# Norms through one root per token, and a modulation summed on VectorE, in a two-block transformer kernel

## The reference

```python
def rmsnorm(x, g):
    y = x * rsqrt(mean(x * x, axis=-1) + EPS)
    return y * g

mod = silu(c) @ w_ada.T + b_ada               # 6 x 1024 values, w_ada is 6144 x 1024
sh1, sc1, gt1, sh2, sc2, gt2 = split(mod, 6)

h = rmsnorm(x, g_mix) * (1 + sc1) + sh1       # norm "first"
proj = h @ w_in                               # q, k, v, pooling, gated convolution
attn = diff_attention(q, k, v)                # 8 heads of 64
attn = rmsnorm(attn, g_subln) * 0.8           # per head: "subln"
x = x + gt1 * (concat(attn, pool, conv) @ w_out)
h = rmsnorm(x, g_ffn) * (1 + sc2) + sh2       # norm "ffn"
x = x + gt2 * (silu(gate) * up) @ w_down
x = rmsnorm(x, g_final)                       # norm "final"

h = rmsnorm(x, g_norm1)                       # norm "second"
# three attentions: fox, swa, and one over 256 memory rows:
mn = rmsnorm(mem, g_mem)                      # norm "mem"
mk, mv = split(mn @ w_mem_kv, 2)
x = x + merged @ w_out_2
x = x + peer_ffn(rmsnorm(x, g_norm2))         # norm "peer", experts picked by top-k
```

## Time and profile before

| | |
|---|---|
| runs, us | 2722.94, 2724.3, 2726.37 (median 2724.3) |
| profiled execution, us | 2727.47, its span 2725.7 |
| TensorE busy | 2557.2 us, 94% |
| VectorE busy | 1528.9 us, 56% |
| ScalarE busy | 725.1 us, 27% |
| GpSimd busy | 1786.2 us, 66% |
| mean granted TensorE clock | 0.970 |

### The profile page before, as it was taken

How to read it: one execution, slowest core, us unless ns; L and a number is a source line. 1 busy time by engine, 2 the same in 40 slices (tenths; PEclk the granted TensorE clock), 3 DMA queues, 4 the chain that set the end, 5 groups by cost and what they waited for, 6 DMA issues and landing times.

```text
span 2725.7 us, 35334 instructions
## 1 busy us (share of the span) xinstructions
PE 2557.2 (94%) x12644; PEld 2132.2 (78%) x12644; DVE 1528.9 (56%) x3197; ACT 725.1 (27%) x1297; POOL 1786.2 (66%) x1315
## 2 busy tenths in 40 slices
PE   3989799999989999998889998999999989999999
PEld 2866568888757666677768898999999978888887
DVE  5447632121246325445438898877778366666665
ACT  5148511000132323433310111111212123333332
POOL 2746557666824243366556676999998668888885
PEclk8989899999989999999999998999999999999999
DMA  6224222222311011122223345899987799999995
GB/s 245 93 70 148 101 77 93 93 103 98 108 48 62 31 47 66 47 92 79 78 81 118 119 146 197 291 366 357 345 337 296 273 365 346 342 341 352 352 353 219
DMA packets 134761, 502.61 MB, mean 184 GB/s; under 512 B 11248, under 2 KB 53872, under 8 KB 103152
## 3 DMA queue, kind: packets, MB, share of 16 engines
q1 hardware_dynamic: 70832, 311.97, 31.4%
q0 software_dynamic: 36864, 134.23, 13.0%
q10 hardware_dynamic: 26944, 54.85, 5.3%
HBM read 448.58 MB, written 52.43 MB: 184 GB/s over the span
## 4 chain that ended last, share of the span: by engine, by line
PE 61%; DVE 11%; POOL 10%; DMA 9%; issue 5%; ACT 3%; ACTq 0%; SPq 0%; DVEq 0%; POOLq 0%
PE banks L566 9%; PE banks L567 9%; PE banks L568 9%; DMA raw<-weights 4%; POOL W_lo L503 3%; POOL W_lo L426 3%; PE banks L694 3%; DMA B_lo_plain<-u_rows,arena 3%; PE banks L924 2%; PE banks L926 2%; PE banks L925 2%; PE banks L839 2%; PE banks L841 2%; PE banks L840 2%; PE banks L712 2%
## 5 line engine op out<-in xcount | busy, mean ns | idle before, releaser
L451 POOL TENSOR_TENSOR W_lo<-raw,W_hi 128x512 fp32r<-128x512 f32 x376 | 493.9, 1323 | 0.0
L454 POOL TENSOR_TENSOR beat<-zero 128x1 f32<-128x1 f32 x94 | 19.8, 211 | 615.8 <-PE banks L714 215.5
L839 PE MATMUL banks<-A_hi,W_hi 128*128 128x384 f32 x1024 | 381.0, 372 | 1.2 <-issue 1.1
L841 PE MATMUL banks<-A_hi,W_lo 128*128 128x384 f32 x1024 | 346.4, 338 | 0.0
L840 PE MATMUL banks<-A_lo,W_hi 128*128 128x384 f32 x1024 | 344.5, 336 | 0.0
L426 POOL TENSOR_TENSOR W_lo<-raw,W_hi 128x2048 fp32r<-128x2048 f32 x65 | 299.4, 4606 | 5.2
L566 PE MATMUL banks<-A_hi,W_hi 128*128 128x512 f32 x680 | 267.8, 394 | 4.9 <-issue 4.9
L568 PE MATMUL banks<-A_hi,W_lo 128*128 128x512 f32 x680 | 264.7, 389 | 0.0
L567 PE MATMUL banks<-A_lo,W_hi 128*128 128x512 f32 x680 | 264.6, 389 | 0.0
L446 POOL CAST W_hi<-raw 128x512 fp32r<-128x512 f32 x376 | 247.9, 674 | 0.0
L1877 DVE TENSOR_TENSOR A_lo<-arena,A_hi 128x768 fp32r<-128x768 f32 x64 | 136.6, 2134 | 171.5 <-ACT A_hi L1362 171.4
(11 more groups left out here) (282 smaller groups left out, 6185.0 us busy)
## 6 DMA issues: line engine op xcount, KB each, us to landing
raw<-weights SPq DMA_DIRECT2D x241, 1024.0 KB, 4.9
gelu_dram<-B_plain ACTq DMA_DIRECT2D x64, 384.0 KB
gates_dram<-arena ACTq DMA_DIRECT2D x48, 512.0 KB, 10.0
arena<-gelu_dram SPq DMA_DIRECT2D x32, 768.0 KB, 8.4
arena<-gates_dram SPq DMA_DIRECT2D x32, 768.0 KB, 11.1
W_plain<-weights SPq DMA_DIRECT2D x4, 1024.0 KB, 15.9
X<-x_t SPq DMA_DIRECT2D x1, 2048.0 KB, 14.4
arena<-v_rows,arena POOLq DMA_INDIRECT x128, 7.9
```

The lines of the kernel that those rows point to most:

```text
L451: return pool.tensor_tensor(W_lo[:, j, cols], raw[:, j, cols], W_hi[:, j, cols].bitcast(F32), ALU.subtract)
L839: mm(to, lh, rh, start=k == 0, stop=False)
L841: last = mm(to, ll, rh, start=False, stop=k == KD - 1)
```

## The change

**Roots.** TensorE now takes the block of 128 tokens of a square as the stationary operand and one column of mean_all as the moving one (`norm_sums`), four matmuls of one column for each of the eight squares: the mean stands once per token, tokens on the partitions, in 128 x 4 values. ScalarE's root and VectorE's reciprocal work on these, in `roots`, a part of `small` in SBUF. `norm_spread` brings them back over features by tokens: the column of a block, broadcast to 128 columns, is stationary, and the identity streams (128 columns). VectorE's products wait for it (`root_spread`). In "mem" the spread stands behind the slab on A. "subln" becomes one such group for all eight heads: 16 matmuls of two columns, one root and one reciprocal of 128 x 32 values, and 32 spreads of 64 x 128, which stand between the two halves of the `behind_split`; VectorE multiplies and splits tile by tile behind them. The other head norms stay.

**First modulation.** All eight slabs have places of their own (four in the arena, two each in B and B_lo) and are issued at once, X behind the first; the first two slabs of w_in follow into raw without a wait. VectorE multiplies a half slab by silu(c), which ScalarE leaves in PSUM, and sums it in the same instruction; ScalarE has no part in it. VectorE's reciprocal of "first" stands before the last slab. The biases are copied to PSUM. The split of w_forget moves behind the norm, the exponential of lambda to the end of the stage before the difference attention. Behind the first spread four matmuls of 512 columns are added that nobody reads (`HEAD_BUSY`).

```diff
+HEAD_BUSY = 4
-        small = sb("small", [P, 56])
+        small = sb("small", [P, 88])
+        roots = small[:, 56:88]
...
+        ada_places = [at(4096 + SLAB * i, SLAB) for i in range(4)] + \
+            [t[:, 4 * i:4 * i + 4, :].rearrange("p a b -> p (a b)") for t in (B_plain, B_lo_plain) for i in range(2)]
+        c_psum = two_banks[0][:, :]
+        def head_root(b, i):
+            return bank[(6, 7, 5 - b, 4 + b)[i]]
...
@@ sync
-            for s in range(2):
-                sp.dma_start(raw[:, s, :], stream[s, :, :]).then_inc(slab_loaded[s], 16)
-            sp.dma_start(X[:, :, :], x_in.rearrange("(k p) t -> p k t", p=P)).then_inc(const_loaded, 16)
-            for s in range(4):
-                sp.dma_start(W_plain[:, s, :], stream[2 + s, :, :]).then_inc(ada_loaded[s], 16)
+            for s in range(ADA_FIRST):
+                sp.dma_start(ada_places[s], stream[s, :, :]).then_inc(ada_loaded[s], 16)
+                if s == 0:
+                    sp.dma_start(X[:, :, :], x_in.rearrange("(k p) t -> p k t", p=P)).then_inc(const_loaded, 16)
-            for s in range(6, ADA_FIRST + 2):
-                sp.wait_ge(ada_used, s - 5 if s < ADA_FIRST else s - 1)
+            for s in range(ADA_FIRST, ADA_FIRST + 2):
                 load_slab(s, s % 2)
@@ tensor
-            def behind_split(which, ks=range(KD), waits=range(KD), n_slabs=1, stride=256):
+            def behind_split(which, ks=range(KD), waits=range(KD), n_slabs=1, stride=256, ahead=None):
...
                 for k in ks:
+                    if ahead and k == waits[0]:
+                        ahead()
...
-            def norm(name):
-                n = NORMS[name][1]
+            def norm_sums(name):
+                blocks = NORMS[name][1] // P
                 b = work()
                 for k in range(KD):
                     take(norm_square)
-                    last = mm(bank[4 + b][:, 0:n], mean_all, S[k % 4][:, 0:n], start=k == 0, stop=k == KD - 1)
+                    for q in range(blocks):
+                        last = mm(bank[4 + b][:, q:q + 1], S[k % 4][:, P * q:P * q + P], mean_all[:, 0:1],
+                                  start=k == 0 and q == 0, stop=k == KD - 1, skip_group_check=True)
                     if k < 4:
                         last.then_inc(square_summed, 1)
                 last.then_inc(work_ready[b], 1)
+                return b, blocks
+
+            def norm_spread(b, blocks):
+                take(root_inverted)
+                for q in range(blocks):
+                    last = mm(bank[4 + b][:, P * q:P * q + P], roots[:, q:q + 1].to_broadcast([P, P]), ident,
+                              start=q == 0, stop=True, skip_group_check=True)
+                last.then_inc(root_spread, 1)
+
+            def norm(name):
+                norm_spread(*norm_sums(name))
...
             norm("first")
+            for _ in range(HEAD_BUSY):
+                mm(bank[2][:, :], mean_all, tab[:, :], start=True, stop=True, skip_group_check=True)
             behind_split("A")
...
-            for _ in head_norm("subln"):
-                pass
-            behind_split("B", ks=(4, 5, 6, 7, 0, 1, 2, 3), waits=range(4))
+            b = work()
+            for i in range(4):
+                take(square_ready)
+                for q in range(QT):
+                    last = mm(bank[4 + b][:, 8 * i + 2 * q:8 * i + 2 * q + 2], S[i][:, P * q:P * q + P], mean_64[:, 0:P:HD],
+                              start=i == 0 and q == 0, stop=True, skip_group_check=True)
+            last.then_inc(work_ready[b], 1)
+            def spread_heads():
+                take(root_inverted)
+                for i in range(4):
+                    for q in range(QT):
+                        for r in range(2):
+                            at_head = 8 * i + 2 * q + r
+                            last = mm(head_root(b, i)[HD * r:HD * r + HD, P * q:P * q + P],
+                                      roots[:, at_head:at_head + 1].to_broadcast([P, HD]), ident,
+                                      start=q == 0, stop=True, skip_group_check=True)
+                    last.then_inc(root_spread, 1)
+            behind_split("B", ks=(4, 5, 6, 7, 0, 1, 2, 3), waits=range(4), ahead=spread_heads)
...
-                    norm("mem")
+                    sums = norm_sums("mem")
                     features_on_partitions("A", 1)
+                    norm_spread(*sums)
                     stage()
@@ scalar
-                act.activation(bank[4 + w % 2][:, 0:n], bank[4 + w % 2][:, 0:n], ACT.Sqrt, bias=small[:, 0:1])\
+                act.activation(roots[:, 0:n // P], bank[4 + w % 2][:, 0:n // P], ACT.Sqrt, bias=small[:, 0:1])\
                     .then_inc(root_ready, 1)
...
-            for s in range(2):
-                modulation(s)
...
-            for s in range(2, ADA_FIRST):
-                modulation(s)
...
+            act.activation(small[:, 4:6], small[:, 2:4], ACT.Exp).then_inc(small_done, 1)
             loaded()
             stage_end()
@@ vector
-                step(dve.reciprocal(root, root))
+                dve.reciprocal(roots[:, 0:n // P], roots[:, 0:n // P]).then_inc(root_inverted, 1)
                 if before:
                     before()
+                take(root_spread)
...
+            def first_modulations(*slabs):
+                for s in slabs:
+                    dve.wait_ge(ada_loaded[s], 16)
+                    for m in range(2):
+                        w = ada_places[s][:, D * m:D * m + D]
+                        dve.scalar_tensor_tensor(out=w, in0=w, scalar=1.0, in1=c_psum, op0=ALU.mult, op1=ALU.mult,
+                                                 accum_out=mod[:, 2 * s + m:2 * s + m + 1])
...
-            head_norm("subln")
-            for i in range(4):
-                dve.drain().then_inc(whole_ready, 1)
-            split(4, lambda i: Ot[:, i, :], "B")
+            take(root_ready)
+            dve.reciprocal(roots, roots).then_inc(root_inverted, 1)
+            for i in range(5):
+                if i < 4:
+                    take(root_spread)
+                    o = Ot[:, i, :]
+                    dve.scalar_tensor_tensor(out=o, in0=o, scalar=small[:, 8 + i:9 + i], in1=head_root(w % 2, i)[:, :],
+                                             op0=ALU.mult, op1=ALU.mult).then_inc(whole_ready, 1)
+                if i >= 1:
+                    rest(i - 1, Ot[:, i - 1, :], "B", 0)
```

More of the change, by code:

```diff
@@ L228, in build @@
         slab_loaded = [sem("slab_loaded0"), sem("slab_loaded1")]
-        ada_loaded = [sem(f"ada_loaded{i}") for i in range(4)]
+        ada_loaded = [sem(f"ada_loaded{i}") for i in range(ADA_FIRST)]
         ada_used = sem("ada_used")
@@ L436, in split_whole, with split @@
                 low_of(s)
-            def split(s, j, ada=N_ADA - 4):
+            def split(s, j, ada=N_ADA - ADA_FIRST):
                 pool.wait_ge(slab_loaded[j], s * 8 + (8 * ada + 16))
@@ L1117, in _ @@
             silu_of_c(1)
-            for s in range(2):
-                modulation(s)
             act.wait_ge(const_loaded, 16 * 3)
             take(small_ready)
-            act.activation(small[:, 4:6], small[:, 2:4], ACT.Exp).then_inc(small_done, 1)
+            squares("first")
+            norm("first")
+            stage_end()
             act.activation(wf_hi[:, :, :], c_("w_forget", 0, 64).rearrange("p (k h) -> p k h", k=KD), ACT.Copy)\
                 .then_inc(small_done, 1)
-            squares("first")
-            for s in range(2, ADA_FIRST):
-                modulation(s)
-            norm("first")
-            stage_end()
             load(dist, "distance")
@@ L1160, in _ @@
             stage_end()
-            for _ in head_norm("subln"):
-                pass
+            for i in range(4):
+                act.activation(S[i], Ot[:, i, :], ACT.Square).then_inc(square_ready, 1)
+            w = at_["work"]
+            at_["work"] += 1
+            act.wait_ge(work_ready[w % 2], w // 2 + 1)
+            act.activation(roots, bank[4 + w % 2][:, 0:32], ACT.Sqrt, bias=small[:, 0:1]).then_inc(root_ready, 1)
             split(4, lambda i: Ot[:, i, :], "B")
@@ L1657, in _ @@
             split(4, lambda i: Kt[:, i, :], "A", followed=False)
+            take(small_done)
+            step(dve.tensor_tensor(small[:, 7:8], small[:, 5:6], small[:, 4:5], ALU.subtract))
+            dve.tensor_scalar(small[:, 6:7], small[:, 7:8], -LAMBDA_INIT, None, ALU.add)
             stage_end()
```

53 lines of the change are left out of this document (24 added, 29 removed).

## The result

The changed kernel took 2734.24 us (median of 20 runs, 2725.74 to 2736.81), the kernel before 2725.39 us (20 runs beside them, 2721.26 to 2727.83). The ratio is 1.0031, its 95% interval 1.0024 to 1.0037: slower by 8.9 us, 0.3%, a little more than the 0.2% that such a measurement can tell. The forecast was +4.8 us and a range of 2700 to 2740; the time lies in it, and the difference is nearly twice the forecast one.

The account below looks back on a forecast made before the run. TensorE, busy 94% of the span, was taken to bound the kernel, with another chain at the head. -11.0 + 0.5 + 5.7 + 3.2 + 11.4 - 5.0 = +4.8 on 2724.3 gave 2729.1 us, range 2700 to 2740.

Parts of the forecast that it names:

- subln: Head norm subln: TensorE's idle time for four reciprocals goes, second half of matmuls starts sooner; -5.0 us.
- the other norms: Norms "ffn", "final" and "peer": dearer sums, shorter work behind them, +1.9 us each; "second", sums at the low clock, +3.2.
- Head, -11.0: Program start: one-pass modulation and earlier weight loads let TensorE start at 41.4 us, -9.9, with -1.1 for the clock.
- the table load: Before the difference attention: the moved exponential adds a table load behind ScalarE's last copy; +0.5 us.
- The clock's -1.1: First slab matmuls at the head: the dummy matmuls, lasting to 40.4 us, raise the clock from 1.2 GHz; -1.1 us.
- Price of the sums: Norm sums on TensorE: each one-column pass costs its weight load, 0.11 us at 2.4 GHz, 0.21 at 1.2 GHz.
- Clock during the sums: Norm sums: the clock falls about halfway through, so they take 10.3 us against 6.9, +3.4.
- the forecast -1.5: Behind a norm's sums: at the low clock 4.3 us from sums to first product become 2.8; -1.5 us.
- Rival A: All new sums: weight loads keep the array counted as busy and the clock up; -20.2 us, 2704 us, chance 0.22.
- "Mem", +11.4: Norm "mem": spread behind a slab makes TensorE wait for VectorE's norm and restart at the low clock; +11.4 us.
- Rival B: Subln: clock stays down through matmuls and spread, +9.4 us for -5.0; 2743.5 us in all, chance 0.13.
- Rival C: Head: dummy matmuls or GpSimd's split end later, -7 us for -11; 2733 us in all, chance 0.10.

Follow-up runs that it names:

- sums64: The changed kernel with 64 equal columns in each pass of the norms' sums in place of one: 2717.39 us.
- best: The changed kernel with 64 equal columns per pass of the norms' sums and the spread of "mem" directly behind its sums: 2707.53 us.
- best_subln32: The kernel of best with 32 columns in place of 2 in each pass of subln's sums: 2708.88 us.
- mem_early: The changed kernel with the spread of "mem" directly behind its sums, ahead of the slab of matmuls: 2724.21 us.
- first_wide: The changed kernel with the norm "first" made as before (512-column sums, no spread), the modulation still changed: 2732.66 us.
- best_no_busy: The kernel of best_subln32 without the four dummy matmuls at the head: 2710.73 us.

## Why the prediction was right, and where its terms were off

**The sign and the size.** +4.8 was forecast and +8.9 measured, by the forecast's own mechanisms: the clock fell in the sums, the wait in "mem" is there, the head and subln gain. Up to the expert stage at 1440 us the ledger has +4.9, but errors cancel in it. That the sum came so near is in part luck. On one side subln gained 4.6 more than forecast, the difference attention 1.4 and "mem" 0.3. On the other the head gained 1.4 less, the other norms cost 3.0 more (1.1, 0.9, 1.0), and 2.1 went in stretches where I had forecast no change.

**Head, -11.0.** The start was right to 0.1 us (41.4), with each step of it: the squares at 17, 64 passes at the low clock to 30.9 (30.6), the split on GpSimd as the releaser. The +0.8 up to the difference attention came all at its start (-9.9 still at 142 us), where the table load was forecast with +0.5. No run shows that term: the eleven other kernels have the same table load, and their change from 133 to 174 us is -0.4 to +1.2. The clock's -1.1 failed: the dummies ended at 37.6, because the clock rose within them (their passes start 0.85 us apart at first, then 0.43), TensorE then idled 3.81 us, and the stretch 40 to 46 has 0.72. The runs sums64, best and best_subln32 show what was meant: their shift is -11.4 to -11.7 at 64 us.

**Price of the sums.** A pass costs its weight load: 0.111 at 2.4 GHz for a forecast of 0.11, 0.21 at 1.2 GHz for 0.21. This was the central number, taken from fp32r matmuls of 128 columns, and it held for one column and for 64. The Trainium skill (TensorE: Matmul & The Clock Gate, section LDWEIGHTS) gives a load as its columns by 1.2 GHz, an estimate of 107 ns for 128. The trace agrees at the high clock; at the low clock it has twice that. For subln's spread I took 0.11 for each of the 64 passes, one behind another; they ran two at a time, a pair every 0.109 us. That is the mis-sized term of subln: 64 passes 3.65 us and not 7.0, which is 3.4 of the 4.6; sums and first half were 1.2 sooner than forecast. It is the pairing that the trace shows, and not that a load of 64 columns by itself costs half: in the difference attention such passes take 0.109 each. No run tested the pairs by themselves.

**Clock during the sums.** I took it to fall halfway, 10.3 us in all. It fell within 3 us: 11.48 in "ffn", 11.40 in "peer". That is +1.1 for each, and all of the miss at these two norms; behind the sums the forecast -1.5 stands at -1.46 (6.67 to 5.21). "Second" took 13.79 for 13.6. Rival A, the clock stays up, fell for this kernel; in sums64, where it did stay up in "ffn", the gain there is the -2.2 that the rival was priced with. That busy time is no guarantee was read rightly from the earlier trace rows: TensorE was busy 7.81 of 8.00 us at half the clock.

**"Mem", +11.4.** Measured 11.1: the slab behind the sums lost 1.8 at the low clock (2.0), the restart 7.4 (7.7; from a shift of -8.3 at the slab to -0.9), what follows it 1.9 (1.7). The run mem_early took 10.0 us back in the times, and 8.1 at this norm in the ledger.

**Rival B** (subln's spread at the low clock) did not happen: the clock was back before the spread, 1.00 from 304 to 308. **Rival C** did not happen by its mechanism: the dummies ended early and GpSimd's split in time (41.40). The head gave 1.4 less than forecast, for the clock and the scatter told above.

**What the forecast had as 0.** Behind "peer" TensorE's slab won 1.4 us, since less of it ran at the low clock. Then the wait for ScalarE grew from the 1.76 of the earlier trace rows to 3.10,

```profile
1426.30 1.13 PE L903 MATMUL banks<-arena 128*128 128x128 f32 x8 [3.10 <-ACT arena L1024]
```

and the clock fell for 3.4 us (0.72 over 1426 to 1432, before 1.00 over 1424 to 1430): +1.5 in all. And the last third, the expert stage, gave +4.0 in the profile, as a sum of losses and gains. The shift is +4.9 at 1440 us, +7.1 at 1800, +7.8 at 2240, +11.9 at 2256, +10.6 at 2309 and +8.8 at 2573. The first step is a longer wait and 3.4 us at the low clock behind it; the same matmul before, then in the changed kernel:

```profile
1790.49 0.49 PE L899 MATMUL banks<-A_lo_plain,A_plain 128*128 128x128 f32 x2 [1.05 <-DVE A_lo_plain L1842]
```

```profile
1796.07 0.80 PE L941 MATMUL banks<-A_lo_plain,A_plain 128*128 128x128 f32 x2 [2.05 <-DVE A_lo_plain L1896]
```

The largest step is at 2252. TensorE there, and the stretch behind the wait:

```profile
2250.16 0.39 PE L968 MATMUL banks<-W_lo,A_hi 128*128 128x512 f32 x1
2252.73 0.50 PE L966 MATMUL banks<-B_hi,A_hi 128*128 128x512 f32 x1 [2.18 <-DVE A_lo L1931]
```

```profile
2254.00:2256.00 2.00, 2.00 (x6) 1.51 (x6) 1.90 (x2) 0.00 (x0) 0.96 (x1) 0.50 1.00 381
```

TensorE waits 2.18 us for VectorE's subtraction and comes back at 1.2 GHz, 4.1 us in all. But 3.0 of these come back by 2573 us, at matmuls where the kernel before waits and the changed one does not, as here:

```profile
2309.15 0.50 PE L924 MATMUL banks<-B_hi,A_hi 128*128 128x512 f32 x1 [0.69 <-DVE A_lo L1877]
```

So that one wait does not explain the +4.0. What the stage adds differs from run to run: from 1440 us to the end the shift changes by -0.6 (first_wide) to +3.1 (best_no_busy) in the eleven other kernels, 1.4 in the mean. Each kernel was profiled once. Whether the 1.4 go with coming to this stage at another moment or with that one profile of the kernel before, and whether the rest of the 4.0 belongs to the changed kernel or to this one execution, stays open.

## What to carry to other kernels

A matmul with few columns costs its weight load, so "one value per token" saves nothing on TensorE by itself; filling the pass with equal columns cost nothing here (0.111 us a pass with 1 and with 64) and kept the clock through the sums of "ffn", "final" and "peer", though not of "second". Where VectorE's work depends on a TensorE instruction, its place among TensorE's instructions decides what hides under what: four passes moved behind one slab cost 10 of the 24 us that the new norms lost. Before taking a change that is slower in sum as useless, keep a ledger by positions of the same instruction: here it had 20 us of gain and 29 of loss in it, and the losses could be undone.

## What the runs showed of the hardware that was not expected

- In "ffn" the granted clock fell within 3 us of one-column passes though matmuls and weight loads fill the time; with 64 columns behind the same loads it stayed at 1.00. In "second" it fell with 64 columns too, and was 0.51 over 734 to 740 with matmuls and loads busy 6.00 of 6.00 us.
- Passes with a stationary operand of 64 columns whose results go in turn to the lower and the upper 64 partitions ran in pairs, two every 0.109 us; into one half they took 0.109 us each.
- At the start of a program the recorded clock can read too high: in the run without dummies it is 1.00 from 40 to 46 us, while 11 matmuls run in the time of 21. The pace of the matmuls tells the clock there.
- VectorE's subtraction of 768 columns (L1931) took 4.72 us in place of 0.95 where a subtraction of GpSimd ran at the same time; the rows of VectorE around the wait of 2252 us, then GpSimd's:

```profile
2247.95 4.72 DVE L1931 TENSOR_TENSOR A_lo<-arena,A_hi 128x768 fp32r<-128x768 f32 x1 [2.46 <-ACT A_hi L1404]
...
2256.04 0.95 DVE L1931 TENSOR_TENSOR A_lo<-arena,A_hi 128x768 fp32r<-128x768 f32 x1
```

```profile
2247.27 4.58 POOL L508 TENSOR_TENSOR B_lo<-raw,B_hi 128x2048 fp32r<-128x2048 f32 x1 [0.56 <-ACT B_hi L1397]
```

VectorE's began 0.68 us into GpSimd's and ended 0.8 behind it, as if it had waited for it. This is no event of the changed kernel alone: of the 64 such subtractions 39 overlap one of GpSimd there and 35 in the kernel before, 18 and 17 take over 4 us, and every one of the 74 ends 0.81 to 0.95 us behind GpSimd's. That holds even for the one at 2236.18, which began 0.42 ahead of GpSimd's and took 5.86. The 54 without an overlap take 0.95 to 0.98. GpSimd's take 4.5 to 4.7 throughout. No run tested the pair by itself. The Trainium skill (GPSIMD Engine Reference, section Specifications) says that the two engines share their way into SBUF and that VectorE's instructions with two SBUF inputs contend there; this subtraction has two, and the trace agrees, with 4.72 us for 0.95.
